# Selection of two score tiles placed inside the query projection, whose token blocks are reordered, and a later load of the MLP residual rows

## What is computed

```python
rel = relu(einsum('bqhd,bld->bqhl', qi, ki) * D_IDX ** -0.5)     # 4 index heads
score = einsum('bqhl,bqh->bql', rel, wi * H_I ** -0.5)
score = where(adm, score, -inf)
_, sel = top_k(score, 256)
```

## Time and profile before

| | us |
|---|---|
| three runs, median (lowest, highest) | 3863.07 (3853.89, 3863.38) |
| profiled execution, its own time | 3851.34 |
| profiled execution, span | 3849.6 |
| TensorE busy | 3513.7 (91% of the span) |
| VectorE busy | 2110.5 (55%) |
| ScalarE busy | 1905.7 (50%) |
| POOL busy | 255.0 (7%) |

### The profile page before, as it was taken

How to read it: one execution, slowest core, us unless ns; L and a number is a source line. 1 busy time by engine, 2 the same in 40 slices (tenths; PEclk the granted TensorE clock), 3 DMA queues, 4 the chain that set the end, 5 groups by cost and what they waited for, 6 DMA issues and landing times. The chain is left out here.

```text
span 3849.6 us, 49950 instructions
## 1 busy us (share of the span) xinstructions
PE 3513.7 (91%) x19049; PEld 2966.2 (77%) x19049; DVE 2110.5 (55%) x3754; ACT 1905.7 (50%) x3006; POOL 255.0 (7%) x426
## 2 busy tenths in 40 slices
PE   8998998985699689998999799999996999999998
PEld 6886786444588578887888588888885888789997
DVE  4334664784466467677666655555554334443334
ACT  2223443776366468776777255565552333332322
POOL 0000010000101110002000100001001000110000
PEclk9998998996799889999999899999998999999999
DMA  5547445650831322333323351111104232422211
GB/s 158 156 141 233 144 152 184 212 152 20 206 81 44 118 102 88 129 132 121 133 106 110 129 155 37 48 38 41 37 7 143 99 109 96 145 74 80 88 66 50
DMA packets 236385, 420.13 MB, mean 109 GB/s; under 512 B 33153, under 2 KB 134145, under 8 KB 227201
## 3 DMA queue, kind: packets, MB, share of 16 engines
q1 hardware_dynamic: 196192, 338.91, 27.5%
q0 software_dynamic: 15776, 66.96, 5.3%
q10 hardware_dynamic: 24192, 11.24, 1.2%
HBM read 336.69 MB, written 80.12 MB: 108 GB/s over the span
## 5 line engine op out<-in xcount | busy, mean ns | idle before, releaser
L1308 PE MATMUL rPV<-rV,rPTr 128*128 128x64 f32 (+1 forms) x2592 | 337.6, 271 | 0.7 <-ACT rPTr L1376 0.7
L1308 PEld LDWEIGHTS rPV<-rV,rPTr 128*128 128x128 f32 x2592 | 326.1, 191 | 10.8 <-issue 1.1
L2497 ACT ACTIVATE gRU<-gUP 128x512 f32<-128x512 f32 (+1 forms) x64 | 41.7, 652 | 498.1 <-PE gUP L2337 498.1
L1360 ACT ACTIVATE rX<-rX,rmx 128x1168 f32<-128x1168 f32 (+7 forms) x128 | 210.6, 1645 | 131.8 <-DVE rmx L1427 131.5
L1376 ACT ACTIVATE rPTr<-rTP 128x512 f32<-128x512 f32 (+1 forms) x360 | 189.3, 553 | 165.0 <-PE rTP L1297 162.2
L2337 PE MATMUL gUP<-gA_hi,gW_hi 128*128 128x320 f32 (+2 forms) x784 | 223.0, 334 | 7.8 <-DVE gW_lo L2539 6.1
L2337 PE MATMUL gUP<-gA_hi,gW_lo 128*128 128x320 f32 (+2 forms) x784 | 222.8, 334 | 0.0
L2337 PE MATMUL gUP<-gA_lo,gW_hi 128*128 128x320 f32 (+2 forms) x784 | 222.7, 334 | 0.0
L2337 PE MATMUL fUP<-fA_hi,fW_hi 128*128 128x512 f32 (+1 forms) x544 | 207.9, 382 | 15.2 <-DVE fW_lo L2539 11.2
L952 ACT ACTIVATE fajunk<-faS,fav 128x2064 int8<-128x2064 f32 (+4 forms) x120 | 205.7, 1714 | 12.0 <-DMA y<-fY 9.7
L2539 DVE TENSOR_TENSOR fW_lo<-fW_raw,fW_hi 128x2048 fp32r<-128x2048 f32 x72 | 163.4, 2291 | 81.3 <-ACT fW_hi L2439 81.3
(11 more groups left out here) (407 smaller groups left out, 8784.7 us busy)
## 6 DMA issues: line engine op xcount, KB each, us to landing
fW_raw<-w_up SPq DMA_DIRECT2D x32, 1024.0 KB, 5.0
fW_raw<-w_down SPq DMA_DIRECT2D x32, 1024.0 KB, 5.1
gW_raw<-w_up SPq DMA_DIRECT2D x32, 1024.0 KB, 5.1
gW_raw<-w_down SPq DMA_DIRECT2D x32, 1024.0 KB, 4.9
qT<-qOUT SPq DMA_DIRECT2D x40, 512.0 KB, 3.3
sKB<-cache_kb SPq DMA_DIRECT2D x8, 2048.0 KB, 9.9
sVB<-cache_vb SPq DMA_DIRECT2D x8, 2048.0 KB, 8.5
kT<-ktz ACTq DMA_DIRECT2D x17, 640.0 KB, 4.4
```

The lines of the kernel that those rows point to most:

```text
L1308: mm = pe.matmul(pv[:, 0:size], PTr[n % 3][:, j - 4 * k, :], V[:, j, a:a + size], start=(j == 0), stop=(j == blk[t] - 1))
L1360: act.activation(X[g % XB][:, 0:n_of[t]], X[g % XB][:, 0:n_of[t]], ACT.Exp, bias=mx[:, g % 4, k:k + 1], scale=-1.0, accum_out=sm[:, g % 4: ...
L2497: act.activation(RU[:, 0:nt * P].rearrange("p (n w) -> p n w", n=n), UP[f % 2][:, 0:n, 0:width], ACT.Relu).then_inc(s_ru, 1)
```

## The change

There are three parts. The order of the token groups in the query projection becomes 0, 3, 2, 1, sample, so that tiles 1 to 3 are scored in the second group, and the last group hosts tiles 4 to 7. Tiles 1 and 2 are selected by turns of ScalarE within `project_queries`: two turns in every step from step 15 on (behind the units of chunks 2 and 6), 50 in all, on a copy of their score rows that POOL makes from `S`. The buffers of these two rows (`rows`) live until the end of the sample attention, where they are closed. The ring of index queries shrinks from 4 to 3. The sample attention keeps tiles 7, 6, 5 on ScalarE and 4, 3 on VectorE, where the two share one buffer, with a new plan. In both feed-forward stages POOL waits for the first piece of `w_o` before it issues the residual rows.

```diff
@@ -412,17 +412,17 @@
-def project_queries(nc, xT, w, gain, scale, rinv, kT, kv, qT, qS, scores, bounds):
+def project_queries(nc, xT, w, gain, scale, rinv, kT, kv, qT, qS, scores, bounds, rows):
...
     BLOCKS = list(range(ABLK, BBLK)) + list(range(0, ABLK)) + list(range(BBLK, QBLK))
-    GROUPS = [(3 * TG, TG), (2 * TG, TG), (TG, TG), (0, TG), (SEQ, P)]
+    GROUPS = [(0, TG), (3 * TG, TG), (2 * TG, TG), (TG, TG), (SEQ, P)]
     NGR = len(GROUPS)
     STEPS = NGR * QBLK
-    XR, RAW, WR, OUTS, QIS, ACCS = 10, 6, 4, 3, 4, 4
+    XR, RAW, WR, OUTS, QIS, ACCS = 10, 6, 4, 3, 3, 4
     FREED = XR - 4
@@ -466,6 +466,8 @@
         scale_sb = sb("scale", [P, QBLK])
+        powers = sb("powers", [P, HALVINGS])
+        limits = sb("limits", [P, HALF])
         acc = [ctx.enter_context(nc.psum_tensor(f"qacc{b}", [P, TG], F32)) for b in range(ACCS)]
@@ -492,6 +494,11 @@
         BD = 4
+        FIRST_TURN = QBLK + QBLK // 2
+        s_pow = sem("s_pow")
+        early = Chain(rows.tiles, rows.S, rows.v, rows.widths,
+                      sb("junk", [P, max(n_of[t] for t in rows.tiles)], mybir.dt.int8), limits, sem("s_pick"),
+                      [sem(f"s_row{i}") for i in range(len(rows.tiles))])
@@ -582,10 +589,15 @@
+            halving_widths(pool, powers, s_pow)
+            most_below(pool, limits, early.tiles, s_pow)
             for j in range(QIS):
...
                 pool.wait_ge(s_bd, BD * j + 2)
+                if t in early.tiles:
+                    i = early.tiles.index(t)
+                    pool.dma_start(early.row(i), S[j % 2][:, 0:n_of[t]]).then_inc(early.s_load[i], 16)
                 pool.dma_start(scores[t * P:(t + 1) * P, 0:n_of[t]], S[j % 2][:, 0:n_of[t]]).then_inc(s_ss[j % 2], 16)
@@ -659,6 +671,15 @@
+            def turn(k):
+                i, h = divmod(k, HALVINGS)
+                if 0 <= i < len(early.tiles):
+                    if k == 0:
+                        act.wait_ge(s_pow, HALVINGS + len(early.tiles))
+                    if h == 0:
+                        act.wait_ge(s_bd, BD * (tiles.index(early.tiles[i]) + 1))
+                    act_bisect(act, early, i, h, powers, bd)
+
             act.wait_ge(s_gain, 16)
@@ -676,6 +697,8 @@
                         relu(u)
+                    if c % 4 == 2:
+                        turn(2 * (s - FIRST_TURN) + c // 4)
                 if gi < NGR - 1:
@@ -700,6 +723,8 @@
                     dve.wait_ge(s_ss[j % 2], 16 * (j // 2))
+                    if tiles[j - 2] in early.tiles:
+                        dve.wait_ge(early.s_load[early.tiles.index(tiles[j - 2])], 16)
                 if u == 0:
@@ -892,13 +917,13 @@
-def picking_plan(sections, act_tiles, act_rows, dve_tiles, dve_rows, lag):
+def picking_plan(sections, act_tiles, act_rows, dve_tiles, dve_rows, lag, early=0):
...
     act_i = act_h = dve_i = dve_h = 0
-    bisected, closed = {}, {}
+    bisected, closed = {("early", i): -1 for i in range(early)}, {}
     closing, mask_free = None, 0
@@ -934,7 +959,7 @@
         dve_plan.append(dve)
-    assert len(closed) == act_tiles + dve_tiles, (len(sections), bisected, closed)
+    assert len(closed) == act_tiles + dve_tiles + early, (len(sections), bisected, closed)
     return act_plan, dve_plan, order, [closed[key] for key in order]
@@ -979,7 +1004,8 @@
     if part == 0:
-        dve.wait_ge(chain.s_pick, (i + 1) * BISECT)
+        if chain.s_pick is not None:
+            dve.wait_ge(chain.s_pick, (i + 1) * BISECT)
         if closed > 0:
@@ -1527,7 +1553,7 @@
 def attend_sample(nc, cache_ka, cache_kb, cache_va, cache_vb, kv, qS, dist, slopes, pick, spread, ident, lambdas,
-                  sub_g, oA, oB, oT, hosted, scores, masks, bounds):
+                  sub_g, oA, oB, oT, hosted, scores, masks, bounds, rows):
@@ -1540,7 +1566,7 @@
     SEL = SEL_FIRST + SEL_STEPS
-    PLAN = [(0, 0)] * 2 + [(2, 4)] * (B - 2) + [(1, 1), (5, 2)] * (B - 2) + [(1, 4), (5, 6)] * 2 + [(6, 7)] * 7 + [(0, 7)]
+    PLAN = [(0, 0)] * 2 + [(2, 4)] * (B - 2) + [(1, 1), (4, 1)] * (B - 2) + [(1, 3), (4, 5)] * 2 + [(4, 5)] * B
@@ -1650,13 +1676,15 @@
         s_store = sem("s_store")
-        on = {kind: Chain(tiles, [sb(f"{kind}S{i}", [P, N_META + P * (tiles[i] + 1)]) for i in range(2)],
-                          [sb(f"{kind}v{i}", [P, 8]) for i in range(2)],
-                          [sb(f"{kind}w{i}", [P, HALVINGS]) for i in range(2)],
+        on = {kind: Chain(tiles, [sb(f"{kind}S{i}", [P, N_META + P * (tiles[i] + 1)]) for i in range(ring)],
+                          [sb(f"{kind}v{i}", [P, 8]) for i in range(ring)],
+                          [sb(f"{kind}w{i}", [P, HALVINGS]) for i in range(ring)],
                           sb(f"{kind}junk", [P, N_META + P * (max(tiles) + 1)], mybir.dt.int8), limits,
                           sem(f"s_{kind}pick"), [sem(f"s_{kind}load{i}") for i in range(2)])
-              for kind, tiles in (("act", hosted[0]), ("dve", hosted[1]))}
-        act_plan, dve_plan, closing, closed_in = picking_plan(PLAN, len(hosted[0]), 2, len(hosted[1]), 2, 1)
+              for kind, tiles, ring in (("act", hosted[0], 2), ("dve", hosted[1], 1))}
+        on["early"] = rows
+        act_plan, dve_plan, closing, closed_in = picking_plan(PLAN, len(hosted[0]), 2, len(hosted[1]), 1, 1,
+                                                                   len(rows.tiles))
@@ -1667,7 +1695,7 @@
                 else:
-                    dve_close(dve, on[kind], i, h, HD, s_close, s_store, closing.index((kind, i)), kind == "act")
+                    dve_close(dve, on[kind], i, h, HD, s_close, s_store, closing.index((kind, i)), kind != "dve")
@@ -1751,9 +1779,8 @@
             most_below(pool, limits, hosted[0], s_pow)
-            for i in range(2):
-                for kind in on:
-                    load_row(pool, on[kind], i, scores)
+            for kind, i in (("act", 0), ("dve", 0), ("act", 1)):
+                load_row(pool, on[kind], i, scores)
             for t in (VB[0][:, PAST // P, :], VB[1][:, PAST // P, :], VA[:, :, PAST // P, :]):
@@ -2284,6 +2311,7 @@
             load_o(0, 1)
+            pool.wait_ge(s_w[0], 16)
             for t in range(NT1):
@@ -2667,7 +2695,8 @@
-EARLY = [7, 6, 5, 4], [3, 2, 1]
+FIRST = [1, 2]
+EARLY = [7, 6, 5], [4, 3]
 LATE = [15, 9, 14, 10, 13], [12, 11, 8]
@@ -2687,9 +2716,15 @@
     project_keys(nc, xT, x, w_keys, attn_gain, ident, idx_norm, kv, kT, rinv)
-    project_queries(nc, xT, w_queries, attn_gain, q_scale, rinv, kT, kv, qT, qS, scores, bounds)
-    attend_sample(nc, cache_ka, cache_kb, cache_va, cache_vb, kv, qS, s_dist, slopes, pick, spread, ident,
-                  lambdas, sub_gain, oA, oB, oT, EARLY, scores, masks, bounds)
+    with ExitStack() as ctx:
+        def sb(name, shape):
+            return ctx.enter_context(nc.sbuf_tensor("e" + name, shape, F32))
+
+        rows = Chain(FIRST, [sb(f"S{t}", [P, N_META + P * (t + 1)]) for t in FIRST], [sb(f"v{t}", [P, 8]) for t in FIRST],
+                     [sb(f"w{t}", [P, HALVINGS]) for t in FIRST], None, None, None, None)
+        project_queries(nc, xT, w_queries, attn_gain, q_scale, rinv, kT, kv, qT, qS, scores, bounds, rows)
+        attend_sample(nc, cache_ka, cache_kb, cache_va, cache_vb, kv, qS, s_dist, slopes, pick, spread, ident,
+                      lambdas, sub_gain, oA, oB, oT, EARLY, scores, masks, bounds, rows)
     attend_prompt(nc, "p", range(0, HALF), kT, kv, qT, masks, p_dist, ident, lambdas, sub_gain, oT)
```

## The result

| | before | after (lowest to highest) | ratio (95%) |
|---|---|---|---|
| first comparison, median | 3863.23 | 3823.57 (3821.49 to 3825.63) | 0.9911 (0.99 to 0.9923) |
| a second comparison of the two, median | 3856.56 | 3826.66 (3823.26 to 3833.83) | 0.9925 (0.9911 to 0.9938) |
| profiled execution, span | 3849.6 | 3823.9 | |

The change makes the kernel faster by 0.75 to 0.9%, that is by 29 to 34 us; the two medians of the first comparison lie further apart, 40 us. By the ratio it is just inside: 0.9911 of 3863.07 is 3829.

What follows compares the result with a forecast made beforehand. TensorE was taken to bound the query projection and first sample-attention jobs, ScalarE's closed chain the last jobs. Terms -27 + 11 + 1 = -15 us gave 3836 profiled, 3848 on the median's scale; range 3828 to 3864.

Steps and rivals of the forecast that it cites:

- Both large terms: Sample attention -27 us from fewer turns, query projection +11 us from the turns moved in.
- the three parts' bounds: Sample attention -33 to -17 us; query-projection turns 0 to +25; residual rows -4.4 to +4.4.
- Part 1, the first jobs: Sample attention: fewer turns gain 0 where TensorE sets the 17.0 us pitch; softmax 9's wait changes by -1.2.
- Part 1, periods: Sample attention from softmax 9: five periods of 11.5 us, then one of 10.7 set by TensorE's loop.
- Part 1, the tail: Sample attention behind softmax 15: 14.4 us loses its four turns, 6.0 us, leaving 8.4.
- Part 2, turns: Query projection: 53.0 us of turns in two heavy blocks overflow 38.5 of free waits, costing +11 us.
- Part 2, the order and the tail: Query projection: reordering blocks costs TensorE 0; the larger last tile's closing maximum and store cost +1 us.
- Part 3: Feed-forward stages: POOL's wait for w_o ahead of the residual rows changes 0 us, bounds -4.4 to +4.4.
- The turns hide altogether: Rival, query projection: eviction waits shrink too, so turns cost nothing; 3837 us, chance 0.16.
- No change: Rival: query stage pays 20 to 25 us, or last sample-attention periods stay at 13 or more; about 3859, chance 0.22.
- Lockstep: Rival, query projection: each heavy-block turn delays relu and TensorE by its whole length; +27 us, 3890, chance 0.09.
- The table switch: Rival, query projection: alternating Relu and Sign costs 100 function-set switches, an estimated 266 us; near 4103, chance 0.02.

Runs made afterwards that it cites:

- The filler: Kernel before with six unread 512-column products in TensorE's wait for ScalarE in each of the last eight sample-attention jobs; ratio 0.9999.
- Behind the last relu: Changed kernel with both turns of a query-projection step behind its last relu instead of behind chunks 2 and 6; ratio 0.9905.
- the later plan: Changed kernel with seven turns instead of five in the first eight sample-attention jobs and two instead of four in later ones; 3815.71 us, ratio 0.9897.

## Why the forecast was half right

The direction and the two stages were right, the size was not: -15 forecast, some -30 measured (35.0 gained, 4.4 paid). Both large terms erred to the same side. The absolute 3848 was also counted from the 3863 of three runs, which was high: the 43 later runs of the kernel before have medians of 3855 to 3857. And the ends of the three parts' bounds add up to -36 and +13, 3827 to 3877, wider than the 3836 to 3857 called the forecast's own range. By its own steps:

- **Part 1, the first jobs, 0.** Softmax 0 to 9 went from 151.0 to 148.5 us, forecast -1.2. The wait of 1.87 went, a turn less stands behind softmax 8, and the product's wait for its keys, which moved a job on and grew, took some back.
- **Part 1, periods.** This is the step that failed most: "five periods (9 to 14) of 15.14 - 2 x 1.82 = 11.5". One of them was (11.46), the others 10.5 to 10.8, and the last 9.04 instead of 10.7. Softmax 9 to 15 took 62.8 us, forecast 68.2, before 88.0. Everything else in the period was taken over as it stood, also ScalarE's wait of 1.84 for the third transpose. That wait contained a value product at 1.2 GHz, and in the shorter periods TensorE entered it at 2.4 GHz in all but the first. The filler shows that the clock alone gives 1.1 us a period. A higher clock stood among the bounds of part 1 (-33), not in its value, and there for TensorE's own loop, not for ScalarE's wait; the 35.0 lie 2 beyond that bound.
- **Part 1, the tail.** 925.28 - 918.19 = 7.1 us, forecast 8.4. The products are at the higher clock here as well (the third copy waited 0.89 us). What ends last is VectorE's closing of tile 5 (to 924.50), with the outputs right behind it; the forecast had looked at the turns and copies only.
- **Part 2, turns.** "Cost: 14.5 - 3.4 = +11": 4.4 measured. The free waits were filled as forecast, 36 of 38.5 us. Two other terms were mis-sized. The turns filled less idle time than 53.0 us: some 47 (36 of free waits, 6.3 of eviction waits, 4.4 by which the blocks grew), as most began 0.1 us before the instruction ahead of them ended. And the eviction gave way by 6.3 us (28.5 + 22.3, the whole of both blocks, to 25.2 + 19.3), where the forecast gave it 3.4. Behind the last relu, it gives way by 36 us more and the cost is 1.8.
- **Part 2, the order and the tail.** +1 forecast, 2.0 measured with the order alone, some 1 by all profiles.
- **Part 3.** 0 forecast, 0 within 3.5 us measured.
- **The rivals.** "The turns hide altogether" was nearest in time (3837), though its reason holds only for another place of the turns. "No change" is out: the late periods went to 10.5, and the query stage paid 4 to 6. Lockstep would have shown 26 us of TensorE's waits for relus: there are 6.4. The table switch is out: the turns stand between relus at 1.15 to 1.26 us a turn, and the whole trace has one ACT_TABLE_LOAD, at 5.5 us.

## What to carry to other kernels

Where a loop between two engines is shortened by taking work from the one, price the other's share again at the clock that it will have then: where a wait contains work at 1.2 GHz, the loop can shrink by more than the work that was taken out (4.6 us a period here for 3.6 of turns). Put added work of an in-order engine behind the instruction that others wait for, and ahead of its own wait (2.6 of 4.4 us here). And before moving work to another stage, see whether the same stage has jobs whose pitch another engine sets: the later plan took 14 us more out of this stage without moving anything out of it.

## What was not expected of the hardware

Six products that nothing reads, put into a wait, made the period of a loop shorter (14.1 to 13.0 us): TensorE took 1.10 us for the eight products behind them and 1.94 without; in two of six periods it took 1.97 in spite of them, and these hardly fell. An unchanged stage, the projection of the keys, differed by 5.3 us between profiles (294.9 to 300.2), about as much as the change cost the query projection, so single stages had to be compared and not the totals of two profiles.
